# Squares and norm weight in the z stage, root factors as diagonals in the transposes, and a split fp32r output projection

## The reference

```python
def rmsnorm(x, w):
    xf = x.astype(jnp.float32)
    y = xf * lax.rsqrt(jnp.mean(xf * xf, axis=-1, keepdims=True) + EPS)
    return (y * w.astype(jnp.float32)).astype(x.dtype)

def ssd_mixer(h, w_in, ..., norm_w, w_out, ...):
    proj = h @ w_in
    z = proj[..., :SSM_INNER]
    ...
    y = y.reshape(b, t, SSM_INNER) * jax.nn.silu(z.astype(f32))
    y = rmsnorm(y, norm_w).astype(h.dtype)
    return y @ w_out, ...
```

## Time and profile before

| | before |
|---|---|
| median of 3 runs | 4682.08 us (4679.7 to 4685.4) |
| the profiled execution | 4693.09 us |
| its span | 4691.4 us |
| PE busy | 4196.0 us (89%) |
| DVE busy | 3264.0 us (70%) |
| ACT busy | 1568.9 us (33%) |
| POOL busy | 1890.4 us (40%) |
| mean granted TensorE clock | 0.94 |

### The profile page before, as it was taken

The page is one execution under the profiler, slowest core; times in us unless marked ns, Lnnn a source line. Parts: engine busy times, 40 slices in busy tenths (PEclk is TensorE's granted clock), DMA queues, the critical chain, the costliest instruction groups (busy, mean ns, idle before and its releaser), DMA issues. The chain is left out here.

```text
span 4691.4 us, 59277 instructions
## 1 busy us (share of the span) xinstructions
PE 4196.0 (89%) x21636; PEld 3722.3 (79%) x21636; DVE 3264.0 (70%) x5837; ACT 1568.9 (33%) x2795; POOL 1890.4 (40%) x1092
## 2 busy tenths in 40 slices
PE   6979989899879999869889789799998996999997
PEld 6868888899868888857777665588888996888886
DVE  4869788799767787836566521227887995788776
ACT  2131333477623232232222220113335774233222
POOL 1213466665444554302111220135666553455441
PEclk8989999999989999989899889899999998999998
DMA  5535466799899999701010010215567998999994
GB/s 190 190 139 201 154 211 206 255 378 366 329 334 356 361 348 350 274 23 44 27 41 27 34 61 36 79 67 192 204 212 288 369 366 317 345 357 352 350 360 159
DMA packets 402070, 1050.10 MB, mean 224 GB/s; under 512 B 23424, under 2 KB 203904, under 8 KB 396800
## 3 DMA queue, kind: packets, MB, share of 16 engines
q1 hardware_dynamic: 289920, 641.57, 38.1%
q0 software_dynamic: 112000, 406.90, 23.8%
HBM read 920.32 MB, written 127.40 MB: 223 GB/s over the span
## 5 line engine op out<-in xcount | busy, mean ns | idle before, releaser
L464 PE MATMUL ov_p<-acts_p,wide_v_p 128*128 128x448 f32 x6144 | 1284.4, 371 | 128.1 <-DVE acts_p L1459 127.9
L464 PEld LDWEIGHTS ov_p<-acts_p,wide_v_p 128*128 128x128 f32 x6144 | 1170.4, 191 | 241.6 <-issue 83.7
L464 PE MATMUL he_p<-h_p,wide_early_p 128*128 128x448 f32 x3456 | 721.9, 370 | 55.3 <-POOL wide_early_p L927 55.1
L464 PEld LDWEIGHTS he_p<-h_p,wide_early_p 128*128 128x128 f32 x3456 | 658.9, 192 | 112.7 <-issue 56.2
L464 PE MATMUL hl_p<-h_p,wide_late_p 128*128 128x448 f32 x2688 | 577.6, 371 | 15.4 <-DVE wide_late_p L1307 15.4
L464 PEld LDWEIGHTS hl_p<-h_p,wide_late_p 128*128 128x128 f32 x2688 | 500.9, 190 | 53.5 <-issue 15.9
L927 POOL TENSOR_TENSOR wide_early_p<-ring,wide_early_p 128x1024 fp32r<-128x1024 f32 x144 | 376.0, 2612 | 321.4 <-ACT wide_early_p L989 321.1
L1430 ACT ACTIVATE acts_p<-hidden_in_p 128x448 fp32r<-128x448 f32 x256 | 148.0, 578 | 849.3 <-DVE hidden_in_p L1455 848.9
L1455 DVE TENSOR_TENSOR hidden_in_p<-hidden_in_p,gbuf_p 128x448 f32<-128x448 f32 x256 | 158.0, 617 | 307.9 <-DMA hidden_in_p<-hidden 307.9
L1177 DVE SCALAR_TENSOR_TENSOR acc_p<-rows_v_p,weight_p,acc_p 128x1024 f32<-128x1024 f32 x286 | 365.6, 1278 | 7.1 <-DVE acc_p L1177 0.5
L1159 POOL DMA_INDIRECT rows_v_p<-in_v,ids_p x160 | 237.7, 1486 | 251.4 <-DVE acc_p L1177 200.4
(11 more groups left out here) (295 smaller groups left out, 6564.9 us busy)
## 6 DMA issues: line engine op xcount, KB each, us to landing
ring<-in_stream SPq DMA_DIRECT2D x162, 2048.0 KB, 11.3
gates<-staged_p SPq DMA_DIRECT2D x28, 2048.0 KB, 7.9
gbuf_p<-gates SPq DMA_DIRECT2D x64, 896.0 KB, 16.4
hidden_in_p<-hidden SPq DMA_DIRECT2D x64, 896.0 KB, 18.7
hidden<-gelu_early_p SPq DMA_DIRECT2D x144, 224.0 KB, 4.3
hidden<-gelu_late_p SPq DMA_DIRECT2D x112, 224.0 KB, 4.8
ada_ineven_in<-in_ada_rows SPq DMA_DIRECT2D x16, 1024.0 KB, 4.9
ada_inq<-in_ada_rows SPq DMA_DIRECT2D x16, 1024.0 KB, 4.9
```

The lines of the kernel that those rows point to most:

```text
L464: last = nc.tensor.matmul(out, lhsT=w, rhs=rhs[:, c, part, cols_], start=start and n == 0, stop=stop and n == 2)
```

## The change

In `gate_by_z`, DVE's loop is written out for all 20 (quarter, tile) steps. After the gating product each step now also sums the squares of its 512 channels into `squares`, and then multiplies them by the norm weight, which comes in as a row repeated on all partitions (`w_row`, 1 MB, loaded by SP at the block's start). In `norm_y` the 20 partial sums are reduced, the root factors are written as five 128 x 128 diagonal matrices `roots`, and the transposes become products of `Y` with these diagonals. Four banks instead of two are used; ACT rounds each result to fp32r and DVE takes the remainder, into `y2`. The output projection is now `project_split` instead of `project`, and `project`, `copy_into` and `add_gated` are deleted.

```diff
-                yT = sb("yT", [P, SSM_INNER // P, TOK], into=ph)
-                norm_y(Y, yT)
-                project("ssd_out", N_SSD_OUT, yT, add_gated(G1, 1), dve_evac=True, chunks=2 * NCH)
+                y2 = sb("y2_ssd", [P, SSM_INNER // P, 2, TOK], F32R, into=ph)
+                norm_y(Y, squares, y2)
+                project_split("ssd_out", N_SSD_OUT, [(y2, part) for part in HALVES], add_gated_halves(G1, 1),
+                              chunks=2 * NCH)
...
                     def _(sp):
+                        sp.dma_start(w_row[:, :], norm_w_rows).then_inc(w_in, 16)
                         feed(sp, first, N_Z)
...
-                        with dve.Fori(0, 2) as r:
-                            for k in range(2 * TILES):
-                                dve.wait_ge(z_out, r * (2 * TILES) + (k + 1 + TILES))
-                                y = Y[:, k % TILES, bass.ds(r * 1024 + (k // TILES) * 512, 512)]
-                                nc.vector.tensor_tensor(y, y, zs[:, k % 2, :], ALU.mult).then_inc(gated, 1)
+                        dve.wait_ge(w_in, 16)
+                        for k in range(4 * TILES):
+                            q, t = divmod(k, TILES)
+                            quarter = slice(q * 512, (q + 1) * 512)
+                            y = Y[:, t, quarter]
+                            dve.wait_ge(z_out, k + 1 + TILES)
+                            nc.vector.tensor_tensor(y, y, zs[:, k % 2, :], ALU.mult).then_inc(gated, 1)
+                            dve.wait_ge(gated, k + 3)
+                            dve_steps.did(nc.vector.tensor_tensor_reduce(
+                                out=junk[:, :], in0=y, in1=y, scale=1.0, scalar=0.0, op0=ALU.mult, op1=ALU.add,
+                                accum_out=squares[:, t, q:q + 1]))
+                            dve_steps.settle(dve)
+                            dve_steps.did(nc.vector.tensor_tensor(y, y, w_row[:, quarter], ALU.mult))
...
-                            v.tensor_scalar(Y[:, t, :], Y[:, t, :], ss[:, t:t + 1], None, ALU.mult).then_inc(scaled, 1)
-                            for b in range(4):
-                                k = 4 * t + b
-                                dve.wait_ge(turned, k + 1)
-                                v.tensor_tensor(yT[:, 4 * b:4 * b + 4, t * P:(t + 1) * P],
-                                                ps[k % 2][:, :].rearrange("p (b t) -> p b t", b=4),
-                                                bcast(col("ssd_norm_w", 4 * b, 4 * b + 4), 2, P), ALU.mult).then_inc(out, 1)
+                            v.tensor_scalar(roots[:, t, :], masks[:, IDENT, :], ss[:, t:t + 1], None, ALU.mult).then_inc(spread, 1)
+                        for k in range(4 * TILES):
+                            dve.wait_ge(his_out, k + 1)
+                            v.tensor_tensor(quarter(k, 1), by_block(k), quarter(k, 0).bitcast(F32), ALU.subtract).then_inc(los_out, 1)
...
                         nc.scalar.activation(ss[:, :], ss[:, :], ACT.Sqrt, bias=eps[:, :], scale=1.0 / SSM_INNER).then_inc(rooted, 1)
+                        for k in range(4 * TILES):
+                            act.wait_ge(turned, k + 1)
+                            nc.scalar.activation(quarter(k, 0), by_block(k), ACT.Copy).then_inc(his_out, 1)
...
+                        for k in range(4 * TILES):
+                            t, b = divmod(k, 4)
+                            pe.wait_ge(spread, t + 1)
+                            if k >= BANKS:
+                                pe.wait_ge(los_out, k - BANKS + 1)
+                            for q in range(4):
+                                last = nc.tensor.matmul(ps[k % BANKS][:, q * P:(q + 1) * P],
+                                                        lhsT=Y[:, t, (4 * b + q) * P:(4 * b + q + 1) * P],
+                                                        rhs=roots[:, t, :], start=True, stop=True)
+                            last.then_inc(turned, 1)
```

More of the change, by code:

```diff
@@ L412, in _ @@
                         adaln_scale(0, SC1)
[L414 to L442, removed]
-                    def evac(eng, steps):
-                        eng.sem_inc(pair_free, 2)
-                        with steps.loop(eng, n_blocks // SLOTS, per_steps) as i:
-                            for o in range(per_round):
-                                eng.wait_ge(blocks_used, i * SLOTS + (first + (o + 1) * each))
-                                evacuate(eng, i * per_round + o, ps[o % 2][:, :], pp[o % 2][:, 0:PROMPT]).then_inc(pair_free, 1)
[L451 to L454, removed]
-                    else:
-                        @block.scalar
-                        def _(act):
-                            evac(act, act_steps)
         def split_matmuls(outs, w_hi, w_lo, moving, c, start, stop):
@@ L1502, in ssd_mixer @@
                 Y = sb("Y", [P, TILES, SSM_INNER], into=ph)
+                squares = sb("squares", [P, TILES, 4], into=ph)
                 with ExitStack() as h_life:
@@ L2054, in _, with norm_y @@
                         dve.sem_inc(gated, 2)
[L2055 to L2061 removed]
+                        dve.wait_ge(w_in, 16)
[11 more added lines that the diff above has]
+                            dve_steps.did(nc.vector.tensor_tensor(y, y, w_row[:, quarter], ALU.mult))
+        def norm_y(Y, squares, y2):
             with ExitStack() as ph:
[L2064 removed]
                 ss = sb("ss", [P, TILES], into=ph)
[L2066 to L2067 removed]
+                roots = sb("roots", [P, TILES, P], into=ph)
+                BANKS = 4
+                ps = [pb(f"pyt{j}", into=ph) for j in range(BANKS)]
+                summed, rooted, spread, turned, his_out, los_out = (
+                    sem("y_" + n) for n in ("summed", "rooted", "spread", "turned", "his_out", "los_out"))
+                quarter = lambda k, part: y2[:, 4 * (k % 4):4 * (k % 4) + 4, part, (k // 4) * P:(k // 4 + 1) * P]
+                by_block = lambda k: ps[k % BANKS][:, :].rearrange("p (b t) -> p b t", b=4)
                 with nc.Block() as block:
@@ L2071, in _ @@
                         v = nc.vector
-                        for t in range(TILES):
-                            dve_steps.did(v.tensor_tensor_reduce(out=junk[:, :], in0=Y[:, t, :], in1=Y[:, t, :], scale=1.0,
-                                                                 scalar=0.0, op0=ALU.mult, op1=ALU.add,
-                                                                 accum_out=ss[:, t:t + 1]))
-                            dve_steps.settle(dve)
-                        dve.sem_inc(summed, 1)
+                        v.tensor_reduce(ss[:, :], squares[:, :, :], AX.X, ALU.add).then_inc(summed, 1)
                         dve.wait_ge(rooted, 1)
```

50 lines of the change are left out of this document (12 added, 38 removed).

## The result

The changed kernel takes 4648.12 us (median of 4 runs, 4641.98 to 4654.7) against 4682.84 us of the kernel before, run beside it: ratio 0.9926, 95% interval 0.9913 to 0.9940. The forecast was 4650, the range 4642 to 4666. The execution that was profiled took 4651.51 us with a span of 4649.9 us, against 4693.09. The total came out almost as forecast, but, as the stages show, from two errors of opposite sign.

The account below looks back on a forecast made before the run. PE bounds the z stage and projection, DVE's sums head `norm_y`, all on the path. 4.1 + 7.2 - 23.6 - 20.3 = -32.6 us from the median 4682.08 gives 4649.5, rounded 4650; range 4642 to 4666.

Parts of the forecast that it names:

- z stage up to the last burst: In the z stage, DVE's longer steps delay ACT's silus and so PE: 4.1 us more, between 2.8 and 11.3.
- last burst: DVE's final z-stage steps have no cover from PE: 10.9 us instead of 3.74, 7.2 us more.
- `norm_y` behind it: Sums and scalings go, diagonal products replace transposes: 17.9 us in place of 41.5, 23.6 less, between 20.4 and 25.6.
- projection: Output projection as 768 fp32r products instead of 256 plain fp32 pairs: 120.3 us instead of 140.7, 20.3 less.
- elsewhere: Stages outside the change: the forecast's sum has no term for them.
- The gap between rounds: Between the two z rounds, ACT's copies, POOL and PE all move by 2.8 us; about 7 in place of 4.47.
- The two stalls of 0.7 inside the rounds: In the z stage, PE's fifth tile waits about 0.7 us for ACT's delayed silu, twice: 1.3 us.
- Rival 1: DVE and POOL collide in the z stage, PE waits: 7.2 us more, 4657 in total; chance 0.18.
- Part 1: The z stage: 4.1 us more, then 7.2 for its uncovered end; POOL's half has 6.9 us of PE time as cover.
- Rival 2: Diagonal products in `norm_y` take four passes, 0.44 us each, 20 groups 35.2 us instead of 14.0: 4671; chance 0.06.
- Ramp: At the projection's start, the first product waits for ACT's copy and POOL's remainder: 4.0 us, before 0.7.
- rival 3: The projection stays at 1.2 GHz, about 226 us, 110 more: 4760 in total; chance 0.03.

Follow-up runs that it names:

- The experiment with transposes: Against the changed kernel, diagonal products became transposes of Y and the root factor was left out of the result; 4647.63 us, ratio 0.9922 to the kernel before.
- the three comparisons: The changed kernel, unaltered, run three times beside the kernel before: 4648.12, 4643.52 and 4645.77 us, ratios 0.9926, 0.9923 and 0.9938.

## Why the prediction was right, and where it was not

By its own steps, in us of the profiled executions:

| step | predicted | measured |
|---|---|---|
| z stage up to the last burst | +4.1 | +3.5 |
| last burst | +7.2 | +6.7 |
| `norm_y` behind it | -23.6 | -17.6 |
| projection | -20.3 | -19.7 |
| sum | -32.6 | -27.1 |
| elsewhere | 0 | -5 to -13 (medians, less the stages) |

* *z stage.* The gap between rounds grew by 7.16 - 4.47 = 2.7 (2.8 predicted). The two stalls of 0.7 inside the rounds came to 0.18 and 0.10; the 0.5 that is left of the 3.5 has no wait in the profile. Rival 1's collision is there, and longer than the earlier trace rows showed, but PE's cover holds, as Part 1 argued.
* *Last burst.* 10.4 against 10.9: a tile is 2.07 where 2.18 was summed, since the next gating product starts 0.61 behind the start of a weight product of 0.69.
* *norm_y, the failed step: the price of the diagonal product.* Ahead of the first product 2.48 us (2.4 predicted). From the first product to DVE's end 2798.01 to 2819.41, 21.4 us, where 14.0 + 1.5 were predicted and 17.2 + 1.5 was the most; the saving of 17.6 lies outside the bounds of 20.4 to 25.6. The prediction took 0.11 us from the earlier trace rows, reading each "x2" as two products. The count of the same line in the kernel before shows what they are:

```profile
L1722 PE MATMUL p_seg<-masks,spans x320: 275/275/422, 2117.6 to 2650.4; 128*128 128x128 f32 x160
```

  8 groups of heads x 5 tiles x 4 heads are 160 products on that line, and 320 instructions: the 0.22 between the rows is the price of one product. The earlier trace rows had it as well: 512 instructions for the projection's 8 x 16 x 2 = 256 products, which the prediction counted as "256 pairs", and 81 in the stretch that holds 80 transposes and the projection's first product. At 0.22 a group is 0.89, above ACT's 0.65, so PE sets the pace: 160 x 0.112 = 17.9, 2.1 more, most of it in the first three us at a clock of 0.50, and 1.4 for the last copy and subtraction. The experiment with transposes shows the same stage at ACT's pace, 13.07.
* *The transpose, beside it.* The prediction read 0.14 for a transpose out of the earlier trace rows, so that a plain product looked no dearer. The row of 1.10 us runs to the end of its last transpose, and one of them lasts 0.27 (the 272 ns of this line of the kernel before):

```profile
L2104 PE MATMUL pyt<-masks,Y x80: 272/421/477, 2807.7 to 2834.1; 128*128 128x128 f32 x80
```

  What counts in a series is the step from one start to the next. From the second to the last of the eight it is 0.109 us (2819.55 to 2820.21, six steps), nearly the 0.112 of one instruction of a product. A plain product thus costs twice a transpose: two instructions instead of one.
* Rival 2 had the right mechanism, more instructions than a transpose, and the wrong factor, two and not four. The Trainium skill, "FP8 and Floating Point Precision", section "TensorE Precision Notes", says that true FP32 takes four passes. In time the trace nearly agrees: an fp32r product of 320 columns takes 115.5/768 = 0.150, so 128 columns would be 0.060 (an estimate by the columns), and 0.224 is 3.7 times that, spread over two instructions. The Trainium skill, "TensorE: Matmul & The Clock Gate", section "Terms", says that the transpose mode is four times faster for FP32. These runs differ: 0.224 is 2.05 times the 0.109 of a transpose.
* *Projection.* Ramp 4.1, products 115.5, end 1.4: 121.0 against 120.3. The clock was 0.97, so rival 3 fell.
* *Elsewhere.* The prediction let nothing outside change. The three stages give 27 to 28.5 us, the medians 32, 35 and 41 in the three comparisons. The difference lies for the most part in layer 1's early expert stage (7.5 us in the mean), and it made up for the mis-sized product. The stages alone would have given 4682.08 - 27.1 = 4655, still in the range; that the total came so near to 4650 is chance, since the prediction had no such term.

## What to carry to other kernels

Before a price is taken from a merged row, count that row's instructions against the products in the code: here 320 for 160 gave away that a plain fp32 product is two. And take the price of one in a series from start to start, since the row's length holds the whole of the last one as well. Where a value is both transposed and scaled, it is cheaper on PE to transpose (13.07 us for the 80 here, against 20.04) and to scale somewhere that already makes a pass. And when a stage is worth less than about 0.2% of the total, measure it by the stage's marks in several profiles, since other stages move by as much from one kernel to the next (402 to 416 us here in one that was not touched).

## What the runs showed that was not expected

* Transposes alone brought the clock up, behind 10.83 us without a product: 0.64 over the first 5.6 us, a mean of the two levels of 1.2 and 2.4 GHz, and 1.00, the higher one, over the next 7.4 (the experiment with transposes). The Trainium skill, "TensorE: Matmul & The Clock Gate", section "Part 4: PE-mode transpose", says that the higher clock does not engage for them; this run differs.
* A DVE instruction beside a POOL elementwise instruction can last nearly as long as that or longer, whatever its own size: 0.18 became 2.29, 0.69 became 2.77. Subtractions with one operand from PSUM did not (0.62 each beside POOL's products); that the operand is the reason was not tested.
* A stage with the same instructions in the same order took 402 to 416 us. The rhythm in which POOL and DVE met in its first 20 us is a part of that; at one rhythm, 4.80, it still took 402.4 to 410.2.
